# Layer zero's output projection: the weight's remainder and seven tiles' products with it ahead of the last tile

## The reference, cut to what matters

```python
def merge(o_a, o_b):
    B, T = o_a.shape[:2]
    return jnp.dot(jnp.concatenate([o_a.reshape(B, T, -1), o_b.reshape(B, T, -1)], axis=-1), w_out)
out_lat = merge(attend(mla_q(...), ka, va), attend(gqa_q(...), kb, vb))
out_ctx = merge(attend(mla_q(...), ka_c, va_c), attend(gqa_q(...), kb_c, vb_c))
# then x = x + gate * out, and an RMS norm for the feed-forward
```

## Time and profile before

| What | Value |
|---|---|
| median of three runs | 2641.23 us |
| profiled execution, whole | 2646.7 us |
| its span | 2644.9 us |
| TensorE matmuls busy | 2579.8 us, 98% |
| VectorE busy | 1383.3 us, 52% |
| ScalarE busy | 928.9 us, 35% |
| GpSimd busy | 369.2 us, 14% |
| mean granted TensorE clock | 0.988 of full |

### The profile page before, as it was taken

One profiled execution on the slowest core, in us unless ns is written; L12 is line 12 of the kernel. 1 busy time (PEld: TensorE's weight loads), 2 busy tenths in 40 slices (PEclk: granted clock), 3 DMA queues, 4 the chain that ended last, 5 costly groups with the idle time before them and its releaser, 6 DMA issues. The chain is left out here.

```text
span 2644.9 us, 32293 instructions
## 1 busy us (share of the span) xinstructions
PE 2579.8 (98%) x13250; PEld 2123.7 (80%) x13250; DVE 1383.3 (52%) x1935; ACT 928.9 (35%) x1282; POOL 369.2 (14%) x270
## 2 busy tenths in 40 slices
PE   7999999999999999999899999999999999999999
PEld 5886666888888888889787888888786788888887
DVE  6325777866368355561485543444785614433332
ACT  4336665242122122352263432332335523322221
POOL 2114532000000000000350000000235343000000
PEclk8999999999999999999899999999999999999999
DMA  6102212423236233122001223223131132223221
GB/s 259 50 30 98 61 41 77 178 96 112 80 134 214 83 130 134 64 80 80 19 1 64 96 71 123 90 73 116 64 112 41 64 108 94 82 85 103 97 86 65
DMA packets 38956, 241.60 MB, mean 91 GB/s; under 512 B 4384, under 2 KB 5408, under 8 KB 15136
## 3 DMA queue, kind: packets, MB, share of 16 engines
q1 hardware_dynamic: 37152, 234.90, 25.0%
q10 hardware_dynamic: 1664, 4.72, 0.7%
HBM read 232.78 MB, written 2.10 MB: 89 GB/s over the span
## 5 line engine op out<-in xcount | busy, mean ns | idle before, releaser
L402 PE MATMUL pair<-h_high,w_high 128*128 128x512 f32 (+1 forms) x1792 | 637.2, 365 | 4.0 <-DVEq L1302 1.6
L403 PE MATMUL pair<-h_low,w_high 128*128 128x512 f32 (+1 forms) x1792 | 634.3, 363 | 0.0
L356 DVE TENSOR_TENSOR w_low<-ring,w_high 128x2048 fp32r<-128x2048 f32 (+5 forms) x164 | 342.1, 2091 | 197.4 <-ACT w_high L332 189.9
L408 PE MATMUL pair<-h_high,w_low 128*128 128x512 f32 (+1 forms) x1792 | 395.6, 363 | 0.0
L332 ACT ACTIVATE w_high<-ring 128x2048 fp32r<-128x2048 f32 (+4 forms) x166 | 288.2, 1737 | 292.3 <-PE pair L408 204.0
L402 PEld LDWEIGHTS pair<-h_high,w_high 128*128 128x128 f32 x1792 | 338.1, 189 | 60.4 <-issue 5.3
L403 PEld LDWEIGHTS pair<-h_low,w_high 128*128 128x128 f32 x1792 | 338.3, 189 | 54.6 <-issue 0.7
L408 PEld LDWEIGHTS pair<-h_high,w_low 128*128 128x128 f32 x1792 | 310.1, 189 | 53.1
L402 PE MATMUL pair<-high,w_high 128*128 128x512 f32 (+1 forms) x704 | 249.1, 363 | 0.8 <-DVE low L1350 0.8
L403 PE MATMUL pair<-low,w_high 128*128 128x512 f32 (+1 forms) x704 | 249.0, 363 | 0.0
L342 POOL CAST w_high<-ring 128x1024 fp32r<-128x1024 f32 x26 | 31.6, 1243 | 1189.0 <-DVE coef L757 703.6
(11 more groups left out here) (512 smaller groups left out, 4096.6 us busy)
## 6 DMA issues: line engine op xcount, KB each, us to landing
ring<-in_w_up SPq DMA_DIRECT2D x66, 1024.0 KB, 4.8
ring<-in_w_ada SPq DMA_DIRECT2D x32, 1024.0 KB, 4.8
ring<-in_w_down SPq DMA_DIRECT2D x32, 704.0 KB, 4.1
ring<-in_w_ada0r SPq DMA_DIRECT2D x16, 1024.0 KB, 4.7
ring<-in_w_merge_b SPq DMA_DIRECT2D x12, 1024.0 KB, 4.8
ring<-in_w_down SPq DMA_DIRECT2D x8, 1024.0 KB, 4.8
ring<-in_w_att_in SPq DMA_DIRECT2D x6, 1024.0 KB, 4.8
ring<-in_w_heads SPq DMA_DIRECT2D x6, 1024.0 KB, 4.8
```

The lines of the kernel that those rows point to most:

```text
L356: op = (on or self.nc.vector).tensor_tensor(self.w_low[:, n % 2, at], self.ring[:, chunk % RING, at], self.w_high[:, n % 2, at].bitcast(F3 ...
L402: self.nc.tensor.matmul(out[:, a:e], w_high[:, k, at], high[:, k, a:e], start=k == 0, stop=False)
L403: self.nc.tensor.matmul(out[:, a:e], w_high[:, k, at], low[:, k, a:e], start=False, stop=False)
L408: mm = self.nc.tensor.matmul(out[:, a:e], w_low[:, k, at], high[:, k, a:e], start=False, stop=k == kt - 1)
```

## The change

For layer zero's projection alone (`LastUnit.apart` is true; it is false in the two other classes that this function serves), four orders change.

- TensorE: ahead of tile n7's products with `w_high`, it waits for the weight's remainder and makes the seven ready tiles' products with it (28 matmuls, new line L1450); behind tile n7 the last four follow (L1469).
- VectorE: five low parts, then the first reciprocal, two low parts, `w_low` of chunk 0, two reciprocals each followed by its scaling, and then the low part of n7.
- ScalarE: the high part of n7 is made in two pieces (`tail`), 512 columns behind the first scaling and 256 behind the second.
- What waits for what else stays the same; the number of TensorE and VectorE instructions is unchanged, and ScalarE has one more.

```diff
+    apart = kt - 1 if last is not None and last.apart else None
@@ TensorE, first_blocks
                 for n, k in enumerate(order):
+                    if n == apart:
+                        pe.wait_ge(K.w_used.sem, first + 1)
+                        for b in range(per):
+                            for a, e in parts:
+                                for j in order[:apart]:
+                                    nc.tensor.matmul(K.pairs[b][:, a:e], w_low[:, j, b * P:b * P + P], high[:, j, a:e],
+                                                     start=False, stop=False)
...
-                        for n, k in enumerate(order):
+                        for n, k in list(enumerate(order))[0 if apart is None else apart:]:
@@ ScalarE
+                    if n == apart:
+                        last.tail(act, high[:, k, :], raw(k)).then_inc(high_ready.sem, 1)
+                        continue
@@ VectorE
+                if n == apart:
+                    K.split_fresh_low(dve)
...
-            if order is not None:
+            if order is not None and apart is None:
                 K.split_fresh_low(dve)
@@ LastUnit
+    def tail(self, act, to, raw):
+
+        for n, (a, e) in enumerate(spans(ALL)):
+            act.wait_ge(self.scaled.sem, self.scaled.base + n + 1)
+            op = self.K.nc.scalar.activation(to[:, a:e], raw[:, a:e], ACT.Copy)
+        return op
@@ LastUnit.dve: the first reciprocal at n == 5 (was 2); the rest at n == KD - 1 (was 3, 4, 5)
```

More of the change, by code:

```diff
@@ L2295 @@
 class LastUnit:
+    apart = True
     def __init__(self, K, inv, mixT):
@@ L2309, in act @@
     def act(self, act, n):
-        if n == KD - 1:
-            act.wait_ge(self.scaled.sem, self.scaled.base + 2)
+        pass
+    def tail(self, act, to, raw):
[3 more added lines that the diff above has]
+        return op
     def dve(self, dve, chain, n):
@@ L2315, in dve @@
         out = self.mixT[rows, self.tile, :]
-        if n == 2:
+        if n == 5:
             dve.wait_ge(self.K.pe_d.sem, self.weighted)
             chain.step(nc.vector.reciprocal(inv[rows, 0:CTX], self.lat[sums, 0:CTX]))
-        if n == 3:
+        if n == KD - 1:
             chain.step(nc.vector.reciprocal(inv[rows, CTX:LAT], self.lat[sums, CTX:LAT]))
@@ L2323, in dve @@
                                     ALU.mult).then_inc(self.scaled.sem, 1)
-        if n == 4:
             chain.step(nc.vector.reciprocal(inv[rows, LAT:ALL], self.ctx[sums, :]))
-        if n == 5:
             chain.sync()
@@ L3433 @@
 class LastHead:
+    apart = False
     def __init__(self, K, floorT, sig, yT, hn, junk, den, ss):
```

## The result

Twelve runs of the changed kernel have a median of 2646.19 us, twelve of the kernel before 2641.07: a ratio of 1.0020, 95% interval 1.0013 to 1.0027. Run again beside other kernels, the ratio was 1.0017 (1.0008 to 1.0027), medians 2645.57 and 2641.29. So the change costs 4.3 to 5.1 us. I had forecast 2643.9, with a range up to 2645.9: the direction was right, the size too small.

A forecast was written before the change was run, and what follows sets the result against it. TensorE was taken as the bound, through when it gets past L995 ahead of block 2. L995's delay 0.3 plus clock 0.7 and 1.7 gave 2.7 us on the median 2641.2: 2643.9 us, 8-in-10 range 2640.7 to 2645.9.

The forecast's parts named there:

- VectorE, ScalarE, TensorE up to the gap: Engine timelines ahead of L995: TensorE's products end 4.1 us earlier, then it idles 4.4 us for ScalarE's square at 473.9.
- Table loads: ScalarE's two table switches before the square: each load followed by its activation after 1.30 us, with no added drain.
- the clock's term: TensorE's clock falls at 471.4 to 472.5 in the gap before L995, two stretches, costing 0.7 + 1.7 us; chance 50%.
- the base: Kernel before: its fall at 459.6 lay ahead of the instant that counts, most of it in waits.
- L995's own delay: TensorE's sums of squares of block 0, ahead of block 2, start 0.3 us later than before, at 473.9 against 473.61.
- The sum: Whole kernel: 0.3 + 0.7 + 1.7 = 2.7 us slower, put on the median 2641.2 as 2643.9 us.
- Small matmuls: L995's small matmuls on TensorE: the fall at 534.7 showed that they do not keep the clock up.
- One stretch: Rival 1, behind the gap before L995: the clock rises after its first stretch; +1.0 us, 2642.2; chance 20%.
- no fall: Rival 2, at the gap before L995: the clock does not fall at all; +0.3 us, 2641.5; chance 10%.
- a faster kernel: Rival 3, at the square: VectorE is last, not ScalarE; TensorE starts 1.15 us earlier, 2640.1; chance 9%.
- three stretches: Rival 4, behind the gap before L995: three stretches at 1.2 GHz; +4.4 us, 2645.6; chance 8%.
- The drain: Rival 5, at ScalarE's table loads: a drain is paid, root 2.8 us later; +5.5 us, 2646.7; chance 1%.

The follow-up runs named there:

- second profile: The changed kernel run again with nothing altered, for another profile: 4.3 us slower than the kernel before, ratio 1.0017.
- Control 1: The kernel before run once more, unaltered, with a profile: timed -0.7 us against the runs of before beside it, ratio 1.0000.
- first profile: The original profile of the kernel before, on which the prediction was built: 2646.7 us whole, span 2644.9.
- controls: The kernel before run twice more, unaltered, each with a profile: one timed at -0.7 us, ratio 1.0000, the other a single run.
- e10: Changed kernel with TensorE's part undone, all 32 products with the weight's remainder behind tile 7 again: +1.8 us against the kernel before, ratio 1.0010.
- e4: Kernel before, without the change, with the squares of block 0 moved behind block 2 in TensorE's queue: +2.2 us, ratio 1.0006.
- e3: Changed kernel with the squares of block 0 moved behind block 2 in TensorE's queue: -1.0 us against the kernel before, ratio 0.9992.
- e1: Changed kernel with 15 more small filler matmuls in TensorE's gap ahead of L995: +1.8 us against the kernel before, ratio 1.0006.
- e2: Changed kernel with ScalarE's series moved ahead of its wait for the last unit's scalings: +2.3 us against the kernel before, ratio 1.0012.

## Why the prediction was too small, step by step

- **VectorE, ScalarE, TensorE up to the gap: right.** Shifted by the 0.18 us, the second scaling ends at 465.8 (465.9 forecast), the tail at 466.3 (466.35), the root at 472.9 (473.0), block 0 is added at 471.6 (471.6), the last four products end at 469.7 (469.55), L995 starts at 473.7 (473.9). The 4.1 us are there and are lost in front of L995.
- **Table loads: right.** 1.30 us from load to activation again, no drain.
- **The first step that failed: the clock's term, too small.** I had two stretches, from 471.4 to 472.5 on, and 0.7 + 1.7 = 2.4 us. It was two stretches, but from 473.7 (472.2 in the second profile, with the stage 0.7 us earlier), so that all or nearly all lay over work: from L995's start to the end of block 2 took 13.03 and 12.71 us against 9.70 in all three profiles of the kernel before, 3.3 and 3.0. I had placed the fall by one other gap, 1.8 us after its start; here it came 4.2 and 3.4 us after the gap's start.
- **The second step that failed: the base.** I wrote of the falls before that "all of that lay ahead of the instant that counts, and most of it in waits", and so put their cost at nothing. But the last 1.2 us of the fall at 459.6 lay over dense work on the way to L995: the tile from 461.81 to 463.85 took 2.04 us where a tile takes 1.39. Control 1 shows the same: from the last wait for a tile to L995 it takes 11.20 us (460.75 to 471.95), the first profile 11.80 (461.81 to 473.61). So the fall had held up L995 by 0.6 us, and the one at 534.7 goes with 1.1 us more by the end of the stretch. The profile that I took as base had itself paid 1.7 us which the two controls did not pay. At 2646.7 us it was slower than every timed run of the kernel before (the highest took 2646.68).
- **L995's own delay.** I charged 0.3 us. Against the profile that I took as base it is 0.08 (24.60 - 24.52), against control 1 it is 0.67: the same row, read from a base that was itself late.
- **The sum.** Against control 1 the stretch is 4.56 us longer: 0.67 for L995, 3.33 for the clock behind the gap, 0.56 behind block 2, where this profile has a fall at 538.5. In the second profile it is 4.62: 0.68, 3.01 and 0.93. Both are near the timed 4.3 to 5.1 us. Against the profile that I took as base it is 2.87 (295.01 - 292.14), close to my 2.7, but that is luck: L995 and the clock give 3.41, and behind block 2 the base's fall at 534.7 cost 0.54 more than the changed kernel's at 538.5.
- **Small matmuls.** From the fall at 534.7 I concluded that "L995 does not keep it up". The row was read rightly, but the controls have the same 24 matmuls and no fall behind them; see the last section.
- **The rivals.** One stretch, no fall, and a faster kernel did not happen; three stretches neither. The drain did not either, though its time, 2646.7, is the nearest: the number agrees, the mechanism does not. I also took it that 5.3 us could hardly be told from no change; with twelve runs of each, 5.1 us stands clear of it.

What stays open: why a fall such as those at 459.6 and 534.7 comes in one execution of the kernel before and not in the others, and how often they come in the timed runs, which have no profile. So how much of the 1.7 us the median of the kernel before pays is not shown. The timed differences and those of the stretch are up to 1.2 us apart, in e10 1.4 and in e4 2.4; I cannot place these parts.

## What to carry to other kernels

Work taken off one engine's path ahead of a wait comes through only if what that wait is for is not made later by the same edit; here the square stood behind ScalarE's tail, and the edit turned 4 us of gain into a gap. Look for the next instruction in the same queue that waits, and move that as well (inside block 2 TensorE had no gap and no fall of the clock in two profiles). And take the base of a sum from more than one profile where the clock is a term: one execution may have paid for falls that others of the same kernel don't have.

## What the runs showed of the hardware

- From this stage to 1100 us the twelve profiles have 26 rows of 24 small matmuls (4 or 2 columns, 2.5 us, TensorE busy): one at the end of this stage, one near 1090, and one more behind block 2 in e3 and e4. In 15 of the 26 the clock fell in the row's last microsecond or within 1.3 us behind it, in 11 it did not. Of the 64 rows of 12 in this stage that stand between dense matmuls without a gap ahead of them, none was followed by a fall. What decides in a row of 24 is not shown.
- With 3.5 us of filler matmuls of 128 columns in the gap, no fall came in the one profile of e1, where both profiles of the changed kernel have one of 6.8 us.
- The stretches of low clock in the twelve profiles lasted 3.4, 6.8, 10.2 or 13.7 us, but for the last of each, which the end cuts off. The three profiles of the kernel before have 62.2, 37.5 and 37.5 us of low clock in all, and spans of 2644.9, 2636.9 and 2637.4 with the same instructions. Of the 8 us between the first and control 1, 6.5 arise around five falls that only the first has (459, 534, 1459, 1828 and 2108 us).
- Two transfers of 512 KB, issued 5.4 us behind a 3 MB reload in e2 (447.8 and 453.2), took 7.4 us to land in the median, and their reader waited until 461.4. In the kernel before they were issued 9.9 us behind it (449.0 and 458.9), when it was nearly over, and took 4.4 us.
